# Laying out all weights on the host by group, one row per partition and one transfer per group

## The reference, cut to what matters

```
first_block:
    proj = rmsnorm(x) @ w_in                 # 1024 x 5384, cut into 13 parts
    ya = rg_lru(conv(lru_x)) * gelu(gate) @ w_out_lru
    yb = sigmoid(m_o) * mlstm(...) @ w_out_mlstm
    yc = stick_breaking_attention(...) @ w_out_sb
    x = x + (sigmoid(g_a)*ya + sigmoid(g_b)*yb + sigmoid(g_c)*yc) @ w_o
    gate, up = split(rmsnorm(x) @ w_ffn_in)  # 1024 x 5632
    x = x + (silu(gate) * up) @ w_ffn_out    # 2816 x 1024
    x = rmsnorm(x)
second_block:
    z = rms_norm(x) @ w_in_2                 # 1024 x 2560
    y = concat(spatial_gating, moba_attention, conformer_conv) @ w_out_2
    x = x + rms_norm(y)
    x = x + rms_norm(cross_attention(x, mem; w_xq, w_xkv) @ w_xo)
    x = x + rms_norm(square(relu(rms_norm(x) @ w_ff1)) @ w_ff2)   # 1024 x 4096, 4096 x 1024
```

## Time and profile before

| | us |
|---|---|
| median of 3 runs (751.32 to 751.40) | 751.38 |
| the profiled execution | 751.22 |
| its span, first to last instruction | 749.5 |
| TensorE busy | 741.8 |
| VectorE busy | 523.3 |
| ScalarE busy | 401.8 |

### The profile page before, as it was taken

One profiled execution on the slowest core, in us unless ns is written; L12 is line 12 of the kernel. 1 busy time (PEld: TensorE's weight loads), 2 busy tenths in 40 slices (PEclk: granted clock), 3 DMA queues, 4 the chain that ended last, 5 costly groups with the idle time before them and its releaser, 6 DMA issues.

```text
span 749.5 us, 10422 instructions
## 1 busy us (share of the span) xinstructions
PE 741.8 (99%) x4300; PEld 650.3 (87%) x4300; DVE 523.3 (70%) x612; ACT 401.8 (54%) x507; POOL 49.3 (7%) x71
## 2 busy tenths in 40 slices
PE   9999999999999999999999999999999999999996
PEld 9988888888988888888899898789988988888885
DVE  4878956895666666666779997885758655556564
ACT  6478378544544544444653685673647443454442
POOL 1100002030000000000230200030003000000000
PEclk9999999999999999999999999999999999999999
DMA  9866465545565555666466436364065566555431
GB/s 332 279 201 225 164 224 195 190 162 174 169 231 172 169 169 183 214 210 204 169 206 220 148 134 225 107 231 167 31 204 168 165 221 223 171 196 191 161 125 57
DMA packets 74095, 138.41 MB, mean 185 GB/s; under 512 B 3900, under 2 KB 28096, under 8 KB 73920
## 3 DMA queue, kind: packets, MB, share of 16 engines
q1 hardware_dynamic: 72192, 132.69, 53.0%
q10 hardware_dynamic: 1856, 5.06, 1.9%
HBM read 136.69 MB, written 1.05 MB: 184 GB/s over the span
## 4 chain that ended last, share of the span: by engine, by line
PE 94%; DVE 2%; DMA 2%; ACT 1%; issue 0%; DVEq 0%; ACTq 0%
PE wide L2045 68%; PE bank L2045 23%; PE bank L2169 2%; DMA raw<-in_w_in_dram 1%; DVE low L1292 1%; DMA arena<-in_x_t_dram 1%; DVE low L1338 0%; DVE arena L1553 0%; ACT high L710 0%; ACT arena L710 0%; DVE act_hl L1334 0%; DVE act_hl L1387 0%; ACT L710 0%; ACT act_hl L710 0%; DVE xn L1781 0%
## 5 line engine op out<-in xcount | busy, mean ns | idle before, releaser
L1292 DVE TENSOR_TENSOR low<-raw,high 128x2048 fp32r<-128x2048 f32 (+1 forms) x118 | 266.8, 2277 | 104.9 <-ACT high L710 100.0
L710 ACT ACTIVATE high<-raw 128x2048 fp32r<-128x2048 f32 (+1 forms) x133 | 234.7, 1782 | 121.6 <-PE wide L2045 97.1
L2045 PE MATMUL wide<-act_hl,high 128*128 128x256 f32 (+1 forms) x1184 | 241.0, 326 | 0.0
L2045 PEld LDWEIGHTS wide<-act_hl,high 128*128 128x128 f32 x1184 | 198.6, 190 | 18.2 <-ACT high L710 0.2
L2045 PE MATMUL wide<-high,act_hl 128*128 128x512 f32 (+1 forms) x560 | 175.8, 388 | 0.5 <-DVE act_hl L1387 0.3
L2045 PE MATMUL wide<-act_hl,low 128*128 128x256 f32 x832 | 162.3, 284 | 0.2
L2045 PEld LDWEIGHTS wide<-act_hl,low 128*128 128x128 f32 x832 | 128.8, 191 | 3.2 <-DVE low L1292 0.4
L2045 PEld LDWEIGHTS wide<-high,act_hl 128*128 128x128 f32 x560 | 104.0, 188 | 23.2 <-issue 1.5
L2045 PE MATMUL wide<-low,act_hl 128*128 128x512 f32 (+1 forms) x280 | 107.4, 384 | 0.0
L2045 PE MATMUL bank<-high,hid_l 128*128 128x512 f32 x216 | 84.4, 391 | 0.2 <-DVE hid_l L1618 0.2
L2045 PE MATMUL bank<-low,hid_h 128*128 128x512 f32 x216 | 84.3, 390 | 0.0
(11 more groups left out here) (207 smaller groups left out, 666.5 us busy)
## 6 DMA issues: line engine op xcount, KB each, us to landing
raw<-in_w_ff_dram SPq DMA_DIRECT2D x32, 1024.0 KB, 5.4
raw<-in_w_in_dram SPq DMA_DIRECT2D x27, 1024.0 KB, 5.2
raw<-in_w_ffn_in_dram SPq DMA_DIRECT2D x44, 512.0 KB, 5.1
raw<-in_w_ffn_out_dram SPq DMA_DIRECT2D x11, 1024.0 KB, 6.6
raw<-in_w_xkv_dram SPq DMA_DIRECT2D x8, 1024.0 KB, 5.1
raw<-in_w_o_dram SPq DMA_DIRECT2D x4, 1024.0 KB, 5.1
raw<-in_w_out_dram SPq DMA_DIRECT2D x4, 1024.0 KB, 5.3
raw<-in_w_xq_dram SPq DMA_DIRECT2D x4, 1024.0 KB, 5.3
```

The lines of the kernel that those rows point to most:

```text
L710: return act.activation(dst, src, func, **k)
L1292: tt(part(low, g), part(raw, g), f32(part(high, g)), SUB).then_inc(sem.low_by_dve, 1)
L2045: return pe.matmul(dst, lhs, rhs, start=start, stop=stop, skip_group_check=loose)
```

## The change

The host now builds one array, `weights`, of 124 groups by 128 partitions by 2048 numbers. The row of a partition holds that group's slices one behind the other, in the order in which the raw tile holds them. `plan_weights` names its sources by string instead of by tensor, so that the host can call it too. The kernel no longer receives the 14 matrices. Each group behind the first three is one transfer from a row of up to 8 KB per partition; the first three are still loaded in slices of 2 KB per partition, now out of those rows. `arrived` counts one transfer for each group. For `ifsv` (width 264) the source row is 4,224 bytes, while the tile keeps its pitch of 512 numbers per slice. Nothing changes for x, x_t, mem, mem_t, gains, the small weights, or on the engines that compute.

```diff
         def arrived(g):
-            return 16 * sum(len(groups[i][0]) for i in range(g % RAW, g + 1, RAW) if i >= FINE)
+            return 16 * sum(i >= FINE for i in range(g % RAW, g + 1, RAW))
...
                 if g >= RAW:
                     sp.wait_ge(low_sem(g - RAW), before(g - RAW))
-                tile = part(raw, g)
+                tile, src, n = part(raw, g), w["weights"][g, :, 0:nk * width], nk
                 if g < FINE:
-                    (src, row, n, d, c, cw), = dmas
                     for k in range(n):
-                        sp.dma_start(tile[:, k, :], src[row + k * P:row + (k + 1) * P, c:c + cw])\
+                        sp.dma_start(tile[:, k, :], src[:, k * width:(k + 1) * width])\
                           .then_inc(first_in[g * n + k], 16)
...
-                for src, row, n, d, c, cw in dmas:
-                    sp.dma_start(tile[:, 0:n, d:d + cw],
-                                 src[row:row + n * P, c:c + cw].rearrange("(k p) n -> p k n", p=P))\
-                      .then_inc(raw_in[g % RAW], 16)
+                sp.dma_start(tile, src.rearrange("p (k n) -> p k n", k=nk)).then_inc(raw_in[g % RAW], 16)
...
 def laid_out(np, inputs):
...
+    groups, _ = plan_weights()
+    arrays["weights"] = np.zeros((len(groups), P, GROUP), np.float32)
+    for g, (parts, _, nk, width) in enumerate(groups):
+        tile = arrays["weights"][g, :, 0:nk * width].reshape(P, nk, width)
+        for name, row, n, d, c, cw in parts:
+            tile[:, :, d:d + cw] = one(name)[row:row + n * P, c:c + cw].reshape(n, P, cw).transpose(1, 0, 2)
+        arrays["weights"][g, :, 0:nk * width] = tile.reshape(P, nk * width)
```

More of the change, by code:

```diff
@@ L49, with plan_weights @@
 DW_ROWS = 2 * DW_TAPS
-def plan_weights(w):
+def plan_weights():
     groups, chunks = [], {}
@@ L65, in add @@
         chunks[key] = ids
-    win = w["w_in"]
+    win = "w_in"
     for key, cols in (("lru", [(0, 0, 512)]), ("qk", [(0, 512, 512)]), ("ifsv", [(0, 1536, 8), (8, 2056, 256)]),
@@ L73, in plan_weights @@
     for b, name in enumerate(("w_out_lru", "w_out_mlstm", "w_out_sb")):
-        add(("branch", b), w[name], 0, 2, [(0, 0, D)], D)
+        add(("branch", b), name, 0, 2, [(0, 0, D)], D)
     for key, row in (("wo_top", 0), ("wo_bottom", 4 * P)):
         for c in range(2):
-            add((key, c), w["w_o"], row, 4, [(0, c * NB, NB)], NB)
+            add((key, c), "w_o", row, 4, [(0, c * NB, NB)], NB)
     n1 = F1 // 256
@@ L80, in plan_weights @@
         if c < n1:
-            add(("up1", c), w["w_ffn_in"], 0, KD, [(0, c * 256, 256), (256, F1 + c * 256, 256)], NB)
+            add(("up1", c), "w_ffn_in", 0, KD, [(0, c * 256, 256), (256, F1 + c * 256, 256)], NB)
         if c >= 1:
-            add(("down1", c - 1), w["w_ffn_out"], (c - 1) * 256, 2, [(0, 0, D)], D)
+            add(("down1", c - 1), "w_ffn_out", (c - 1) * 256, 2, [(0, 0, D)], D)
     def add_kv(c):
-        add(("kv", c), w["w_xkv_2"], 0, KD, [(0, c * NB, NB)], NB)
+        add(("kv", c), "w_xkv_2", 0, KD, [(0, c * NB, NB)], NB)
     add_kv(0)
     for key, c in (("zc", 2048), ("q2", 512), ("k2", 1024), ("za", 0), ("v2", 1536)):
-        add(key, w["w_in_2"], 0, KD, [(0, c, NB)], NB)
+        add(key, "w_in_2", 0, KD, [(0, c, NB)], NB)
     for c in range(1, 3):
@@ L94, in plan_weights @@
         for c in range(2):
-            add((key, c), w["w_out_2"], row, 4, [(0, c * NB, NB)], NB)
+            add((key, c), "w_out_2", row, 4, [(0, c * NB, NB)], NB)
     add_kv(3)
     for c in range(2):
-        add(("xq", c), w["w_xq_2"], 0, KD, [(0, c * NB, NB)], NB)
+        add(("xq", c), "w_xq_2", 0, KD, [(0, c * NB, NB)], NB)
     for c in range(2):
-        add(("xo", c), w["w_xo_2"], 0, KD, [(0, c * NB, NB)], NB)
+        add(("xo", c), "w_xo_2", 0, KD, [(0, c * NB, NB)], NB)
     n2 = F2 // NB
@@ L103, in plan_weights @@
         if c < n2:
-            add(("up2", c), w["w_ff1_2"], 0, KD, [(0, c * NB, NB)], NB)
+            add(("up2", c), "w_ff1_2", 0, KD, [(0, c * NB, NB)], NB)
         if c >= 1:
-            add(("down2", c - 1), w["w_ff2_2"], (c - 1) * NB, 4, [(0, 0, D)], D)
+            add(("down2", c - 1), "w_ff2_2", (c - 1) * NB, 4, [(0, 0, D)], D)
     return groups, chunks
@@ L254, in two_blocks @@
 def two_blocks(nc, w, out):
-    groups, chunks = plan_weights(w)
+    groups, chunks = plan_weights()
     n_groups = len(groups)
@@ L517, in _ @@
         def _(sp):
-            for g, (dmas, view, nk, width) in enumerate(groups):
+            for g, (_, _, nk, width) in enumerate(groups):
                 if g == FINE - 1:
@@ L2605, in _ @@
                         products(("down2", c - 1), "F", c - 1, first=c == 1, last=False)
-_INS = ["x", "w_in", "w_out_lru", "w_out_mlstm", "w_out_sb", "w_o", "w_ffn_in", "w_ffn_out", "final_norm_g", "mem_2",
-        "w_in_2", "gate_ln_g_2", "gate_ln_b_2", "w_out_2", "post_mix_g_2", "w_xq_2", "w_xkv_2", "w_xo_2", "post_x_g_2",
-        "w_ff1_2", "w_ff2_2", "post_ffn_g_2"]
+_INS = ["x", "final_norm_g", "mem_2", "gate_ln_g_2", "gate_ln_b_2", "post_mix_g_2", "post_x_g_2", "post_ffn_g_2"]
 def laid_out(np, inputs):
```

## The result

The changed kernel takes 752.44 us, median of 22 runs (751.59 to 753.40), against 751.27 for the kernel before in as many (751.06 to 751.58): 1.17 us more, ratio 1.0016 with a 95% interval of 1.0010 to 1.0022. The forecast was 751.1 with a range up to 752.0, so the time went the other way and out of the range. The profiled execution took 752.53 us with a span of 750.8; that of before took 751.22.

The account below looks back on a forecast made before the run. PE was taken as the bound, with a weight landing costing it only 0.31 us, ahead of group 3. 751.22 - 0.3 = 750.9, plus 0.16 for the median of the runs, gave 751.1 us; range 750.1 to 752.0.

Parts of the forecast that it names:

- What bounds the kernel: Whole kernel: PE busy 741.8 of 749.5 us; a weight landing costs it time only before 25.60 us, 0.31 us.
- Fewer transfers, longer rows behind 26 us: Weight loads after 26 us: 121 transfers for 145, pieces up to 8 KB; 0 on the path, hidden by 11.7 us of room.
- The estimate of 48 us for exposed fixed costs: 24 fewer transfers at about 2.0 us fixed cost each, if exposed; the forecast said the trace hides it.
- Group 3: Second half of "qk", awaited by PE near 25 us: 8 KB pieces land sooner, -0.31 us, bounds -0.31 and +0.3.
- The first three groups: Twelve opening loads of 256 KB in 2 KB pieces, row pitch from 21.5 KB to 8 KB: taken as 0.
- The nearest row: x_t's opening loads, also 2 KB pieces at 8 KB pitch: 5.2 us to landing against 6.4, used to take 0.
- The lower bound: First twelve loads: the stretch 2 to 3 us moves only 98 GB/s, which rows packed into less memory might shorten.
- The upper bound of +1.7 us: First twelve loads: 3.15 MB at 322 GB/s instead of 391 would land group 3 1.7 us later.
- The rival D: First 24 us: rows at exactly 8 KB pitch meet in the same part of HBM; 753.1 us, at half rate 759.5; chance 0.06.
- The signs: Packets some 24,000, PE busy 741 to 742, smaller gap before group 3, weight waits within 36 us, feed-forward landings under 7 us.
- the two signs of D: PE's first real matmul clearly later than 7.20 us, or a PE gap of over 1 us near 25.

Follow-up runs that it names:

- the layout without gaps: Changed kernel with the first twelve slices one behind the other, 256 KB each, pitch 2 KB: 751.07 us; with group 3 in 2 KB pieces as well, 751.86.
- The early table: Kernel before, plus one small ScalarE activation ahead of its first wait, so that its table loads while x_t is on its way: 751.32 us, ratio 1.0001.
- the reverse in the kernel before: Kernel before, with only the first three groups read from 8 KB rows of a small 3 MB array: 751.83 us, ratio 1.0009.

## Why the prediction was wrong

*What bounds the kernel.* Right for the kernel before, and more so than I used it: PE resumes when group 3 has landed, and whatever moves that moment goes to the end, down to the point where PE is bound by its own matmuls. What the text missed is that the start is a second such place in a slower kernel: PE's own point is 0.85 us later in the changed one (26.10 against 25.25).

*Fewer transfers, longer rows behind 26 us.* Right: nothing, with the packets, the landings and PE's rhythm as described. The estimate of 48 us for exposed fixed costs played no part. It took its 2.0 us from a section of the Trainium skill ("Anatomy of one DMA" in "DMA: Bandwidth & Descriptors") that gives them for transfers issued from GpSimd, and these are issued by SyncE; here whole stores of 256 KB, issued by SyncE, took 2.0 us to land.

*Group 3.* The faster pieces are there (414 and 384 GB/s for 388 and 353), but the gain of 0.31 us did not show. Undoing the first three groups alone should have given 0.31 less than before and gave 0.10, within the noise. With the first three groups in 8 KB rows, the long rows behind them (752.44) did not do better than the short ones (751.83). Group 3's landing took 10.7 us in 8 KB pieces, in the change and with the first groups from w_in, against 10.4 before. Only on the layout without gaps are 8 KB pieces ahead of 2 KB pieces, by 0.79, and that comparison has the doubt named above. The early table in the kernel before shows that even the issue does not move the landing: issued 0.32 us sooner, it ended at the same time. That fits a landing that is set by what is queued ahead; the runs do not show it directly.

*The first three groups: the step that failed.* The text took 0 for them, and the measured cost is 0.6 (the reverse in the kernel before) to 1.3 us (752.44 against 751.14). The nearest row was x_t's landing, 5.2 us at an 8 KB pitch against 6.4 for the weights. That was a poor neighbour: three loads in the same mixed stream, each timed from its issue with others ahead of it in the queue, which says little on the pitch. In the changed kernel these three take 6.2 us, and x_t's first part, loaded through ScalarE's queue, lands 0.85 us later, though x_t's layout is the old one. That PE's first real matmul hangs on x_t's first part and not on a weight was true, and no protection: slow weight loads make x_t late. The lower bound had a true observation in it, and it did not help: from 2 to 3 us the change moves 242 GB/s where the kernel before moves 98, but from 3 to 4 us it moves 187 for 302. The upper bound of +1.7 us for this very step was in the text, and held the result; that the bound was of the right size is partly luck, since its rate of 322 GB/s came from another stretch and not from a row at this pitch. The range was then drawn to 752.0 as if the bound were a remote case. The rival D, with its place, its price of 1.7 us and the remark that it decides from the first percent, is what happened, except that the power of two is not the point: 8,448 and 9,216 bytes lose as well.

*The chance.* D had 0.06. Against it stood only that one row, and for it that DMA is saturated exactly where the pitch changes and that the path runs through it. With no row on a weight at the new pitch it deserved several times that.

*The signs.* Packets, PE's busy time (742.1), the landings in the first feed-forward stage (6.5 us at most), ScalarE's waits for weights (none after 36 us) and the stages behind 40 us (0.12 us at most) came out as the forecast said. The wait ahead of group 3 grew, to 0.69 us. Of the two signs of D the first came, PE's first real matmul at 8.05; the gap of over 1 us did not.

## What to carry to other kernels

Where a new layout keeps the size of the pieces but changes the distance between them, the rate can change, and a saturated start hands it straight to the end: give loads that are issued in small parts an array of their own without gaps (751.07 us here), or try 32 bytes of padding (751.33). Long rows for the loads issued whole did no harm here, and no good that could be shown. Before crediting a quicker start, find the landing that releases the first full stretch of matmuls and ask whether that moves too. When the time minus that moment is constant over several kernels, the cause lies ahead of it, and the rest of the kernel need not be searched. A load whose own layout is unchanged is no safe neighbour to reason from, as long as it is in flight beside those that change.

## What had not been expected of the hardware

With 2 KB pieces for the first twelve loads and x_t as it was, kernels with a row pitch of 8,192, 8,448 or 9,216 bytes moved 213 to 266 GB/s from 2 to 6 us, and those with 8,224, 21,536 or 2,048 bytes 280 to 304. Slow loads on SyncE's queue made unchanged ones on ScalarE's queue late: x_t's first part landed after 4.80 us instead of 3.95. Windows in which later groups came in 8 KB pieces ran above those with 2 KB pieces, with the same first loads (404 against 388 GB/s from 14 to 18 us, 385 against 353 from 18 to 22), and this bought no time that could be told from noise. The changed kernel also scatters more: 751.59 to 753.40 in 22 runs, against 751.06 to 751.58.
